# Transposing the squared MLP activations with VectorE blocks and 16 small DMAs instead of TensorE

## The reference

```python
h = rms_norm(x, pre_mlp_g[l])
m = jnp.square(jax.nn.relu(h @ w_up[l])) @ w_down[l]     # w_up 2048 x 8192, w_down 8192 x 2048
x = x + rms_norm(m, post_mlp_g[l])
```

## Time and profile before

| what | value |
|---|---|
| median of 3 runs | 1093.58 us (1093.05 to 1094.3) |
| the profiled execution, first to last instruction (span) | 1093.7 us |
| PE busy | 1079.3 us, 99% |
| DVE, ACT, POOL busy | 664.7 us, 512.5 us, 97.4 us |
| DMA queue q1 (all of SP's) | 58.1% of 16 engines' span |
| mean granted TensorE clock | 0.997 |

### The profile page before, as it was taken

How to read it: one execution, slowest core, us unless ns; L and a number is a source line. 1 busy time by engine, 2 the same in 40 slices (tenths; PEclk the granted TensorE clock), 3 DMA queues, 4 the chain that set the end, 5 groups by cost and what they waited for, 6 DMA issues and landing times.

```text
span 1093.7 us, 13589 instructions
## 1 busy us (share of the span) xinstructions
PE 1079.3 (99%) x5002; PEld 899.1 (82%) x5002; DVE 664.7 (61%) x706; ACT 512.5 (47%) x655; POOL 97.4 (9%) x104
## 2 busy tenths in 40 slices
PE   8999999999999999999999999999999999999996
PEld 7888888888888788888888888888888888888885
DVE  6455565558975765565565655656646556565566
ACT  6564445545544564444444444443444444444443
POOL 0010121120000530000000000000000000000003
PEclk9999999999999999999999999999999999999999
DMA  9765455454756456565564665655656556466552
GB/s 341 244 220 193 149 170 175 147 185 152 272 194 194 150 193 192 192 192 183 188 191 167 197 192 189 190 186 197 192 192 192 184 188 192 165 196 194 186 191 77
DMA packets 103904, 207.39 MB, mean 190 GB/s; under 512 B 3648, under 2 KB 9408, under 8 KB 103104
## 3 DMA queue, kind: packets, MB, share of 16 engines
q1 hardware_dynamic: 103728, 206.91, 58.1%
q10 hardware_dynamic: 144, 0.04, 0.0%
HBM read 204.84 MB, written 2.10 MB: 189 GB/s over the span
## 4 chain that ended last, share of the span: by engine, by line
PE 95%; DVE 2%; POOL 1%; ACT 1%; issue 1%; DMA 1%; SPq 0%; DVEq 0%; POOLq 0%; ACTq 0%
PE ps L596 30%; PE ps L598 30%; PE ps L597 30%; PE ps L604 3%; DVE w_lo L1153 1%; DMA raw<-in_w_in 1%; PE ps L787 0%; PE ps L841 0%; PE ps L792 0%; DVE xT_lo L1350 0%; ACT u_sb L975 0%; POOL x_res L1565 0%; PE ps L813 0%; PE ps L814 0%; PE ps L812 0%
## 5 line engine op out<-in xcount | busy, mean ns | idle before, releaser
L1153 DVE TENSOR_TENSOR w_lo<-raw,w_hi 128x1024 fp32r<-128x1024 f32 (+2 forms) x383 | 471.1, 1237 | 377.4 <-ACT w_hi L890 376.6
L890 ACT ACTIVATE w_hi<-raw 128x1024 fp32r<-128x1024 f32 (+2 forms) x383 | 397.4, 1039 | 489.1 <-PE ps L598 485.1
L596 PE MATMUL ps<-w_hi,xT_hi 128*128 128x512 f32 (+1 forms) x800 | 314.9, 394 | 4.0 <-DVE xT_lo L1210 2.6
L598 PE MATMUL ps<-w_lo,xT_hi 128*128 128x512 f32 (+1 forms) x800 | 309.8, 387 | 0.0
L597 PE MATMUL ps<-w_hi,xT_lo 128*128 128x512 f32 (+1 forms) x800 | 309.6, 387 | 0.0
L596 PE MATMUL ps<-w_hi,yT_hi 128*128 128x512 f32 x672 | 263.0, 391 | 0.0
L598 PE MATMUL ps<-w_lo,yT_hi 128*128 128x512 f32 x672 | 261.7, 389 | 0.0
L597 PE MATMUL ps<-w_hi,yT_lo 128*128 128x512 f32 x672 | 261.6, 389 | 0.0
L596 PEld LDWEIGHTS ps<-w_hi,xT_hi 128*128 128x128 f32 x800 | 150.6, 188 | 36.1 <-DVE w_lo L1153 3.5
L598 PEld LDWEIGHTS ps<-w_lo,xT_hi 128*128 128x128 f32 x800 | 150.6, 188 | 30.7
L597 PEld LDWEIGHTS ps<-w_hi,xT_lo 128*128 128x128 f32 x800 | 150.8, 189 | 28.4
(11 more groups left out here) (147 smaller groups left out, 428.1 us busy)
## 6 DMA issues: line engine op xcount, KB each, us to landing
raw<-in_w_up SPq DMA_DIRECT2D x64, 1024.0 KB, 5.3
raw<-in_w_down SPq DMA_DIRECT2D x64, 1024.0 KB, 5.0
raw<-in_w_in SPq DMA_DIRECT2D x28, 1024.0 KB, 5.3
raw<-in_w_o SPq DMA_DIRECT2D x16, 1024.0 KB, 5.1
raw<-in_w_uq SPq DMA_DIRECT2D x8, 576.0 KB, 3.9
raw<-in_w_ukv SPq DMA_DIRECT2D x4, 1024.0 KB, 5.1
raw<-in_w_in SPq DMA_DIRECT2D x7, 512.0 KB, 8.5
raw<-in_w_in SPq DMA_DIRECT2D x4, 640.0 KB, 6.9
```

The lines of the kernel that those rows point to most:

```text
L596: nc.tensor.matmul(dst, x_hi, hi, start=first, stop=False)
L598: mm = nc.tensor.matmul(dst, x_hi, lo, start=False, stop=last)
L890: nc.scalar.activation(w_hi[:, slot, 0:size], raw[:, raw_slot, first:first + size], ACT.Copy).then_inc(hi_ready, 1)
L1153: nc.vector.tensor_tensor(w_lo[:, slot, 0:size], raw[:, raw_slot, first:first + size], f32(w_hi[:, slot, 0:size]), ALU.subtract).then_inc( ...
```

## The change

TensorE no longer transposes the squared activations. In place of step 3:

- DVE transposes 32x32 blocks of `a_sb` into `a_blk` (`turn_blocks`, two STREAM_TRANSPOSE instructions of 128x512 a strip), and adds one to `a_turned`;
- SP moves the groups of 32 partitions to their places, `aT_raw` <- `a_blk`, by 16 dma_starts a strip (`move_blocks`), each of 32 partitions by 1 KB, that is 32 KB, and 512 KB a strip. All add to `aT_landed`, 256 a strip. They stand in SP's own instruction order between two quad loads: SP waits there for `a_turned`, issues 16, and goes on with the loads.
- `hidden_hi` and `hidden_lo` read `aT_raw` in SBUF in place of PSUM, through views that reorder (c, g, i) with runs of 32 elements. `hidden_hi` waits for `aT_landed`.

ACT's next relu waits for `a_turned` in place of `aT_filled`. The steps `aT` (now ACT and DVE alone) of strips 0 and 15 move from after the second quad to after the third, and a step `a_turn` stands after the first.

```diff
-        if q == 1:
+        if q == 0:
+            steps.append(("a_turn", 0, 0))
+        if q == 2:
             steps.append(("aT", 0, 0))
...
+            def move_blocks(turned):
+
+                sp.wait_ge(a_turned, turned)
+                for g in range(4):
+                    for q in range(4):
+                        sp.dma_start(aT_raw[BLK * q:BLK * (q + 1), g], a_blk[BLK * g:BLK * (g + 1), q]
+                                     ).then_inc(aT_landed, 16)
...
+                if n == NQ - 3:
+                    move_blocks(1)
             with sp.Fori(LOOP.start, LOOP.stop) as j:
                 for i in range(8):
...
                     load_quad(i % RAW, src)
+                    if i == 2:
+
+                        sp.wait_ge(aT_lo_ready, j - 1)
+                        move_blocks(j)
...
+                if n in (NQ_TAIL + 2, NQ_TAIL + 10):
+
+                    j = FF_STRIPS - (2 if n == NQ_TAIL + 2 else 1)
+                    sp.wait_ge(aT_lo_ready, j)
+                    move_blocks(j + 1)
...
-            def hidden_transposes(j, used=True):
-
-                pe.wait_ge(a_ready, j + 1)
-
-                if used:
-                    pe.wait_ge(aT_lo_ready, j)
-                for tb in range(TB):
-                    mm = transposes(2 + tb, [a_sb[:, tb, c * P:(c + 1) * P] for c in range(4)])
-                mm.then_inc(aT_filled, 1)
...
             def hidden_hi(j, at=0):
-                act.wait_ge(aT_filled, j + 1)
+                act.wait_ge(aT_landed, (j + 1) * 256)
                 for tb in range(TB):
-                    ins = nc.scalar.activation(yT_hi[:, at:at + 4, tb * P:(tb + 1) * P],
-                                               ps[:, 2 + tb].rearrange("p (c t) -> p c t", c=4), ACT.Copy)
+                    ins = nc.scalar.activation(turned(yT_hi, at, tb), blocked(tb), ACT.Copy)
                 ins.then_inc(aT_hi_ready, 1)
...
+            def turn_blocks(j, moved):
+
+                dve.wait_ge(a_ready, j + 1)
+                if moved is not None:
+
+                    dve.wait_ge(aT_landed, moved)
+                for tb in range(TB):
+                    ins = nc.vector.transpose(a_blk[:, :, tb].rearrange("p q c i -> p c q i"),
+                                              a_sb[:, tb].rearrange("p (c q i) -> p c q i", c=4, q=4))
+                ins.then_inc(a_turned, 1)
...
                              base + (i + AHEAD + 1))
+                    if i == 9:
+                        turn_blocks(j, j * 256)
                 hidden_lo(j)
```

More of the change, by code:

```diff
@@ L46 @@
 CHUNK = 64
+BLK = 32
 EPS = 1e-6
@@ L230, in plan @@
         steps.append(("add", q, n))
+        if q == 0:
+            steps.append(("a_turn", 1, 0))
     steps.append(("aT", 1, 0))
@@ L240, in plan @@
         tail.append(("add", 4 * (j - 1) + q, n))
-        if q == 1:
+        if q == 0:
+            tail.append(("a_turn", j, 0))
+        if q == 2:
             tail.append(("aT", j, 4))
@@ L346, in hybrid_block @@
         a_sb = tensor(ctx, "a_sb", [P, TB, W])
+        a_blk = tensor(ctx, "a_blk", [P, 4, TB, 4, BLK])
+        aT_raw = tensor(ctx, "aT_raw", [P, 4, TB, 4, BLK])
         gained = tensor(ctx, "gained", [P, TB, W])
@@ L398, in hybrid_block @@
         relu_ready, a_ready = sem("relu_ready"), sem("a_ready")
-        aT_filled, aT_hi_ready, aT_lo_ready = sem("aT_filled"), sem("aT_hi_ready"), sem("aT_lo_ready")
+        a_turned, aT_landed = sem("a_turned"), sem("aT_landed")
+        aT_hi_ready, aT_lo_ready = sem("aT_hi_ready"), sem("aT_lo_ready")
         acc_added = sem("acc_added")
@@ L498, in hybrid_block, with turned, blocked @@
         RESIDUAL_QUAD = min(n for n, z in quads.items() if z["kind"] == "out") + 2
+        def turned(tile, at, tb):
+            return tile[:, at:at + 4, tb * P:(tb + 1) * P].rearrange("p c (g i) -> p c g i", g=4)
+        def blocked(tb):
+            return aT_raw[:, :, tb].rearrange("p g c i -> p c g i")
         def up_bank(j):
@@ L853, in step @@
                                            for t0 in range(tokens.start, tokens.stop, P)]).then_inc(hT_filled, 1)
-                elif what == "aT":
-                    hidden_transposes(a, used=a > 0)
             for what, a, b in steps:
@@ L876, in _ @@
                     down_quad(i, base + (8 + 2 * i), (j - 1) * 4 + (i + 1))
-                hidden_transposes(j)
             for what, a, b in tail:
@@ L1090, in step @@
                     if a:
-                        act.wait_ge(aT_filled, a)
+                        act.wait_ge(a_turned, a)
                     relu_out(a, 2 * b + 2, up_bank(a))
@@ L1172, in hidden_lo @@
                 for tb in range(TB):
-                    dst = (slice(None), slice(at, at + 4), slice(tb * P, (tb + 1) * P))
-                    ins = nc.vector.tensor_tensor(yT_lo[dst], ps[:, 2 + tb].rearrange("p (c t) -> p c t", c=4),
-                                                  f32(yT_hi[dst]), ALU.subtract)
+                    ins = nc.vector.tensor_tensor(turned(yT_lo, at, tb), blocked(tb), f32(turned(yT_hi, at, tb)),
+                                                  ALU.subtract)
                 ins.then_inc(aT_lo_ready, 1)
+            def turn_blocks(j, moved):
[6 more added lines that the diff above has]
+                ins.then_inc(a_turned, 1)
             def add_down(i, done, added):
@@ L1354, in step @@
                     ins.then_inc(hT_lo_ready, 1)
+                elif what == "a_turn":
+                    turn_blocks(a, 256 * a if a else None)
                 elif what == "aT":
```

## The result

Faster, by less than forecast: 1088.33 us median (4 runs, 1087.26 to 1089.74) against 1093.67 us. The ratio is 0.995, 95% interval 0.9939 to 0.9962, that is 4.2 to 6.7 us. The forecast was 1080.5 us with a range up to 1087.5; the time lies 0.8 us outside.

A forecast was written before the change was run, and what follows sets the result against it. PE alone was taken to bound the MLP. 1093.7 less 14.4 for transposes, nothing in the loop, plus 1.2 and 0.1 at the ends gave 1080.6, or 1080.5 us for the median; range 1078.9 to 1087.5.

The forecast's parts named there:

- What the change removes: On PE, the transposes of all 16 strips: 0.90 us a strip, 14.4 us in all.
- The loop costs nothing: In the loop's 14 strips, the added work on DVE, SP and ACT stays hidden: nothing added.
- The ends: PE's waits before the first down quads: a stall of 0.1 us at strip 0 and 1.2 us at strip 15.
- the issue of a move: SP's price for issuing one of a strip's 16 moves: 0.47 us, with 0.37 as lower bound.
- The landing: Time for a move to land: 3.1 us, with bounds of 1.5 and 5.3 us.
- rival A: SP's moves: issues cost 0.6 to 0.95 us each, still hidden in the loop; 1087.5 us at 0.7; chance 0.12.
- my signs of being wrong: Issues over 0.7 us apart, landing over 5, two block transposes over 2.5, or PE waiting in the loop for `w_hi`, `w_lo`, `yT_lo`.
- Rival B: SP becomes the bound in the loop: beyond 0.96 us an issue strips stall; about 1220 us at 1.5; chance 0.09.
- the splits' lead: In the loop, splits run ahead of PE: 5.8 us, counted for the moves' landing.
- the loads' slack: In the loop, SP's next load may be issued 11.1 us late without stalling PE.
- Rival C: PE's time in the MLP isn't given back, another wait standing just behind the transposes: 1093.5 us; chance 0.06.

The follow-up runs named there:

- The filled stalls: Changed kernel plus 9 and 13 matmuls of no use before PE's waits at strips 0 and 15: 1084.96 us.
- two queues: Changed kernel with ACT issuing 8 of the 16 moves on its own queue at strips 0 and 15: 1087.92 us.
- smaller and larger: Changed kernel plus ten DMAs behind each iteration's moves (one of 32 KB, one of 256 KB, eight of 16 KB): 1088.49 us, one run.
- thirty-two issues: Changed kernel plus sixteen more copies to a spare tile behind each iteration's moves, which nothing waits for: 1095.83 us, one run.
- strip 15 alone earlier: Changed kernel with only strip 15 turned and moved earlier, strip 0 unchanged: 1081.77 us.
- four forms: Changed kernel plus four DMAs behind each iteration's moves, from HBM or SBUF, 32 or 128 partitions, to a spare tile: 1089.03 us, one run.

## Why the prediction was wrong, point by point

**What the change removes: right.** 0.90 us a strip was read from the distances of starts and came back to the hundredth: 44.42 to 43.52 us an iteration. The 272 ns of each transpose would have promised 35 us.

**The loop costs nothing: right.** No wait of PE from 440 to 1028 us (busy 588.0 of 588), block transposes of 1.30 us for two (forecast 1.28), `hidden_hi` 1.14 in place of 1.06, `hidden_lo` the same as from PSUM. The Trainium skill, "VectorE: DVE Perf Modes", section "The three transpose paths", has 311 ns for 128x128 in bf16; here two instructions, together 128x1024 of float32, took 1.30 us, 163 ns for each 128 columns, so the row I had taken was the better price.

**The ends: the step that failed.** "PE stalls 1.2 us" and "stall 0.1 us" were 3.09 and 2.05. The term mis-sized is the issue of a move, taken as 0.47 us from the first loads and measured as 0.63 in the loop and 0.66 to 0.67 at the ends; 15 such distances make the last move start 10 us behind the first and not 7.05. The landing went the other way, 1.9 us for 3.1. Issuing 3.0 us longer less landing 1.2 us shorter is 1.8, and both stalls are 1.9 us longer than forecast. That is rival A's mechanism, which I gave 0.12, with a price inside its 0.6 to 0.95 us. It is luck that the time lies only 0.8 us outside the range: the landing priced too high made up for 1.2 us at each end. And none of my signs of being wrong came true (issues over 0.7 us apart, a landing over 5 us, block transposes over 2.5 us, a wait in the loop); they left the stretch from 0.47 to 0.7 us unwatched, and the clock.

The Trainium skill, "DMA: Bandwidth & Descriptors", section "Anatomy of one DMA", gives about 2.0 us fixed for each DMA on the GpSimd path. The 1.9 us of SP's moves are of that size, and they overlap: the next move is issued 0.63 us later.

**A term that was not in the sum at all.** Each stall was priced as its own length. PE came out of both at the lower clock and paid 1.7 and 2.9 us more, 4.6 of the 8.5 us by which the ends were underrated. The filled stalls show that the clock fell for the standing still. All stalls over 1 us from 395 to 1066 us, in the changed kernel and the experiments, and what the 31 intervals behind each took above 0.227 us:

| stall, us | where | lost behind it, us |
|---|---|---|
| 1.86 | two queues, strip 0 | 0.17 |
| 2.04 | smaller and larger, strip 0 | 1.75 |
| 2.05 | changed kernel, strip 0 | 1.69 |
| 2.21 | thirty-two issues, strip 0 | 1.68 |
| 2.35 | strip 15 alone earlier, strip 0 | 1.71 |
| 2.45 | four forms, strip 0 | 1.72 |
| 2.50 | thirty-two issues, first iteration | 0.13 |
| 3.03 | thirty-two issues, strip 15 | 2.99 |
| 3.09 | changed kernel, strip 15 | 2.92 |
| 3.28 | smaller and larger, strip 15 | 1.70 |
| 3.55 | four forms, strip 15 | 1.69 |
| 3.89 | two queues, strip 15 | 2.73 |

The loss is some 1.7 us or 2.7 to 3.0, and not the longer for a longer stall; 1.86 and 2.50 us had no slow matmul behind them, 2.45 had. So the length of the stall alone doesn't decide it; what else does stays open. With the stalls and the low clock as measured, the sum is 1093.6 - 14.4 + 5.1 + 4.6 = 1088.9 us.

**Rival B was priced from the wrong point.** Not 0.96 but some 1.25 us an issue is where the loop begins to stall, since the splits' lead adds to the loads' slack: with thirty-two issues the load went out 20.4 us after the first move and PE lost 0.35 us, so that about 20.1 us, 16 times 1.25, were free. Rival C is out: the distance of matmuls is 0.227 us beside the moves as before.

## What to carry to other kernels

Where work leaves the bound engine for a longer path, the steady loop hides it and the first and last round, with no other round's work to lie beside, pay: draw their timelines as carefully as the loop's and start the new path there as early as its input allows, or keep the old path for these rounds. Price a stall of TensorE of two microseconds or more as its length and the matmuls at half clock behind it: in ten of the eleven seen here these cost 1.7 to 3.0 us more. A DMA has a price on the engine that issues it, on SyncE here 0.37 to 0.67 us with little regard to its size; sixteen in a row are a stretch of ten microseconds in which that engine does nothing else, and moving them to a busy engine moves the stall.

## What was not expected of the hardware

- Stalls of 2.05 and 3.09 us, the engine at full clock and busy before, brought TensorE down to 1.2 GHz for 9 and 14 matmuls; one of 2.50 us in another run did not (granted clock 1.00 from 459.6 to 464 us):

```profile
456.96 0.39 PE L646 MATMUL ps<-w_lo,xT_hi 128*128 128x512 f32 x1
459.69 0.50 PE L644 MATMUL ps<-w_hi,xT_hi 128*128 128x512 f32 x1 [2.34 <-DVE w_lo L1187]
460.02 0.39 PE L645 MATMUL ps<-w_hi,xT_lo 128*128 128x512 f32 x1
```

(PE in the kernel of thirty-two issues: 2.73 us from start to start, then 0.33 and 0.23. In the kernel with four forms the slow matmuls came only after the first six intervals at nearly full pace.)

- Issues of DMAs back to back: 0.42 us at 16 KB, 0.51 to 0.59 at 32 KB, 0.58 at 256 KB, 0.37 for a load of 1 MB. Two queues at once were no cheaper an issue: at strip 0 SyncE's eight took 5.56 us, 0.70 each, and ScalarE's 6.50, 0.81 each. GpSimd issued four in 2.20 us, 0.55 each, and they landed in about 1.8 us.
- A STREAM_TRANSPOSE of 128x512 float32 through views with runs of 32 takes 0.69 us, as a two-input pass of the same size.
